# Order of the recurrent blocks, and where the prompt's expert rows stand, in a one-core hybrid diffusion step

## The reference, cut to what matters

```python
def trunk_layer(x, cond, p, cache):
    sh_a, sc_a, g_a, sh_f, sc_f, g_f = adaln(cond, p['w_ada'], p['b_ada'])
    h = rmsnorm(x, p['norm_attn_g']) * (1.0 + sc_a) + sh_a
    q, k, v, xr, xg, ga, gr = jnp.split(h @ p['w_in'], IN_SPLITS, axis=-1)
    ...
    rnn, hf_last, hb_last = rglru_branch(xr, ...)
    a_out = attn @ p['w_attn_o']
    r_out = (rnn * jax.nn.gelu(xg)) @ p['w_rnn_o']
    mix = (jax.nn.sigmoid(ga) * a_out + jax.nn.sigmoid(gr) * r_out) @ p['w_out']
    x = x + g_a * mix
    h = rmsnorm(x, p['norm_ffn_g']) * (1.0 + sc_f) + sh_f
    return x + g_f * peer(h, ...), k, v, hf_last, hb_last

def rglru_dir(xc, w_a, b_a, w_i, b_i, lam, h0, reverse):      # once forward, once backward
    r = jax.nn.sigmoid(blockdiag(xf, w_a) + b_a)
    ig = jax.nn.sigmoid(blockdiag(xf, w_i) + b_i)
    log_a = -LRU_C * r * jax.nn.softplus(-lam)
    a = jnp.exp(log_a)
    bterm = jnp.sqrt(-jnp.expm1(2.0 * log_a)) * ig * xf
    _, h = lax.associative_scan(_lin_combine, (a, bterm), axis=1)

# peer: per token 8 heads x 16 experts = 128 slots
act = gelu(einsum('chkd,cd->chk', u_tab[eidx], x))            # one dot product per slot
out = einsum('chk,chkd->cd', g * act, v_tab[eidx])            # one weighted row per slot
```

## Time and profile before

| what | value |
|---|---|
| median of the runs | 2470.72 us |
| profiled execution | 2466.62 us |
| its span in the profile | 2464.7 us |
| VectorE busy | 1873.9 us (76%) |
| TensorE busy | 1785.5 us (72%) |
| GpSimd busy | 1041.1 us (42%) |
| ScalarE busy | 514.6 us (21%) |
| moved by DMA | 753.43 MB, mean 306 GB/s |

### The profile page before, as it was taken

The page is one execution under the profiler, slowest core; times in us unless marked ns, Lnnn a source line. Parts: engine busy times, 40 slices in busy tenths (PEclk is TensorE's granted clock), DMA queues, the critical chain, the costliest instruction groups (busy, mean ns, idle before and its releaser), DMA issues.

```text
span 2464.7 us, 20335 instructions
## 1 busy us (share of the span) xinstructions
PE 1785.5 (72%) x6013; PEld 1085.0 (44%) x6013; DVE 1873.9 (76%) x3933; ACT 514.6 (21%) x1283; POOL 1041.1 (42%) x1028
## 2 busy tenths in 40 slices
PE   7788889889987989991334666689999997000185
PEld 3578754444456438450012333556666664000032
DVE  2342388875689466899999999888687987999955
ACT  0464113550024000110004555720000000000111
POOL 0000001224534341443775766344344447777674
PEclk9889999999998999996556777899999998555599
DMA  8766774557855595765997999689999999999997
GB/s 278 250 196 209 253 215 149 162 171 268 313 198 187 199 336 168 284 229 201 397 409 290 391 392 387 201 317 411 414 411 406 410 408 411 410 409 410 369 401 308
DMA packets 296873, 753.43 MB, mean 306 GB/s; under 512 B 21502, under 2 KB 141102, under 8 KB 296244
## 3 DMA queue, kind: packets, MB, share of 16 engines
q0 software_dynamic: 147456, 536.94, 57.6%
q1 hardware_dynamic: 149308, 215.20, 24.9%
HBM read 740.72 MB, written 11.33 MB: 305 GB/s over the span
## 4 chain that ended last, share of the span: by engine, by line
DVE 37%; PE 26%; DMA 17%; POOL 8%; issue 7%; ACT 5%; SPq 1%; DVEq 0%; ACTq 0%; POOLq 0%
PE bank L779 8%; PE pair L779 6%; DMA ring_more<-in_peer_u_dram,eidx 6%; DVE attn L1530 5%; DVE big L1530 4%; ACT work L1080 3%; PE bank L960 3%; DVE ring_more L1530 3%; PE bank L1008 3%; POOL attn L2089 2%; DMA attn<-in_peer_u_dram,eidx 2%; POOL big L2089 2%; PE bank L752 2%; DMA big<-in_peer_u_dram,eidx 2%; DMA h_all<-in_peer_u_dram,eidx 2%
## 5 line engine op out<-in xcount | busy, mean ns | idle before, releaser
L1008 PE MATMUL bank<-big,work 128*128 128x512 f32 x192 | 123.9, 781 | 392.9 <-ACT work L1080 269.5
L2089 POOL DMA_INDIRECT h_all<-in_peer_u_dram,eidx x117 | 129.7, 1108 | 569.9 <-DVEq L1958 366.2
L779 PE MATMUL pair<-big 128*128 128x128 f32 (+1 forms) x1280 | 359.3, 438 | 5.1 <-issue 3.6
L779 PE MATMUL bank<-big 128*128 128x512 f32 (+1 forms) x1056 | 312.3, 457 | 20.3 <-DVEq L1399 13.6
L2089 POOL DMA_INDIRECT attn<-in_peer_u_dram,eidx x205 | 201.8, 984 | 238.5 <-DVE dots L1530 167.7
L1053 PE MATMUL bank<-h_all,big 128*128 128x512 f32 x608 | 267.0, 595 | 4.5 <-DMA h_all<-in_peer_v_dram 4.5
L1530 DVE CUSTOM_DVE_ANT_0 attn<-attn,pair 128x1024 f32<-128x1024 f32 x205 | 244.0, 1219 | 32.8 <-DMA attn<-in_peer_u_dram,eidx 28.8
L779 PEld LDWEIGHTS pair<-big 128*128 128x128 f32 x1280 | 196.8, 194 | 154.7 <-issue 152.5
L2089 POOL DMA_INDIRECT ring_more<-in_peer_u_dram,eidx x145 | 156.1, 1077 | 208.6 <-DVE dots L1504 100.1
L1008 PEld LDWEIGHTS bank<-big,work 128*128 128x128 f32 x192 | 41.8, 237 | 456.6 <-issue 419.0
L779 PEld LDWEIGHTS bank<-big 128*128 128x128 f32 x1056 | 173.6, 206 | 154.2 <-issue 146.8
(11 more groups left out here) (310 smaller groups left out, 3020.2 us busy)
## 6 DMA issues: line engine op xcount, KB each, us to landing
big<-in_w_in_dram SPq DMA_DIRECT2D x44, 1024.0 KB, 6.3
h_all<-in_peer_v_dram SPq DMA_DIRECT2D x76, 512.0 KB, 6.8
big<-in_w_ada_dram SPq DMA_DIRECT2D x24, 1024.0 KB, 8.9
big<-in_peer_w_q_dram SPq DMA_DIRECT2D x16, 1024.0 KB, 5.8
gf_row<-in_peer_v_dram SPq DMA_DIRECT2D x26, 512.0 KB, 6.8
work<-in_peer_v_dram SPq DMA_DIRECT2D x26, 512.0 KB, 6.8
big<-in_w_rnn_o_dram SPq DMA_DIRECT2D x8, 1024.0 KB, 6.4
big<-in_w_attn_o_dram SPq DMA_DIRECT2D x8, 1024.0 KB, 6.9
```

The costliest lines, as they stand in the source:

```text
L779: last = nc.tensor.matmul(u[:, 0:n], w[:, k, col:col + P], src[:, k, 0:n], start=(k == 0), stop=(k == KD - 1))
L1008: last = nc.tensor.matmul(psum[i][:, :], diag[:, (n - 1) % DIAGS, :], ring[r][:, i * 512:(i + 1) * 512], start=(k == first_by_tensor[c]), ...
L2089: g.indirect_dma_start(dst, None, ins["peer_" + table][0], bass.IndirectOffsetOnAxis(ap=eidx[:, c, k:k + 1], axis=0)).then_inc(landed, 16)
```

## The change

Nothing of what is computed changes. Six edits:

1. Prompt phase, TensorE: the gates of block j-1 stand between `xr` and `xg` of block j, no longer behind the ada unit.
2. Prompt phase, buffers: `lru_rows` gives odd and even blocks different halves of the buffers (a prompt block uses 128 of 512 columns), so ScalarE's wait for `lru_done` reaches back two blocks, not one.
3. ScalarE: `gelu_in` is split. `gelu_tanh(j + 1)` stands behind the six exp-type instructions of block j in both phases; `gelu_square(j + 1)` moves there too in the prompt phase and keeps its place for the latents.
4. VectorE: the second gelu step becomes `gelu_out`, and stands behind the four products of the block before.
5. Latents, `serve`: two items per recurrent block (before: five, counting the one in `conv`); 7 and not 4 ahead of the recurrent merge, and 9 and not 5 beside each of its steps.
6. Latents, `serve`: none beside the last two queries; 2 + 1 per attention quad (before: 3 + 1).

Of the first 133 items the recurrent stage now does 16, the merge 7 + 72, the queries 12, attention 24, and two are left for `gelu_dots(0)`.

```diff
@@ units
             unit((ph, "xr", j), 2 * (j % 2))
+            if ph == 0 and j:
+                gates(j - 1)
             unit((ph, "xg", j), 2 * (j % 2) + 1)
...
-            if j:
+            elif j:
                 gates(j - 1)
@@ buffers
-        lt, la, le, lth, lti = ([wk(2 + 2 * i), wk(3 + 2 * i)] for i in range(5))
+        def lru_rows(ph, j):
+            c0 = (j % 2) * P if ph == 0 else 0
+            return ([wk(2 + 2 * i + d)[:, c0:c0 + TOK[ph]] for d in range(2)] for i in range(5))
@@ ScalarE
-                    if j + 1 < LB:
-                        gelu_in(j + 1)
+                    if ph and j + 1 < LB:
+                        gelu_square(j + 1)
...
-                    if j:
+                    if ph and j:
                         act.wait_ge(lru_done, B)
+                    if ph == 0 and j >= 2:
+                        act.wait_ge(lru_done, B - 1)
...
+                    if j + 1 < LB:
+                        if ph == 0:
+                            gelu_square(j + 1)
+                        gelu_tanh(j + 1)
                     for d in range(2):
                         act.wait_ge(w_ready, 2 * B + d + 1)
@@ VectorE
-                    serve(1)
+                    serve(0)
+
+                def gelu_out(j):
...
                     if j + 1 < LB:
                         conv(j + 1)
-                    serve(1)
...
-                        serve(1)
+                    serve(1)
+                    if j + 1 < LB:
+                        gelu_out(j + 1)
...
-                        serve(5 if a == "gr" else 5)
-                serve(4)
+                        serve(9 if a == "gr" else 5)
+                serve(7)
...
                         rope((ph, "q", h), featT[:, h, 0:N])
-                        serve(2)
+                        if h < NH - 2:
+                            serve(2)
...
-                    serve(3)
+                    serve(2)
                     dve.wait_ge(prob_ready, G * Q + G)
```

More of the change, by code:

```diff
@@ L370, in hybrid_step @@
         xc = [wk(0), wk(1)]
-        lt, la, le, lth, lti = ([wk(2 + 2 * i), wk(3 + 2 * i)] for i in range(5))
+        assert TOK[0] == P
+        def lru_rows(ph, j):
+            c0 = (j % 2) * P if ph == 0 else 0
+            return ([wk(2 + 2 * i + d)[:, c0:c0 + TOK[ph]] for d in range(2)] for i in range(5))
         sm_pair = [wk(4 * i, 4).rearrange("p (h n) -> p h n", h=G) for i in range(2)]
@@ L1138, in _, with gelu_square, gelu_tanh @@
                     end_stage()
-                def gelu_in(j):
+                def gelu_square(j):
                     u = full((ph, "xg", j))
                     run(featT[:, j, 0:N], u[:, 0:N], ACT.Square).then_inc(sq_ready, 1)
+                def gelu_tanh(j):
                     act.wait_ge(cub_ready, LB * ph + j + 1)
                     run(featT[:, j, 0:N], featT[:, j, 0:N], ACT.Tanh, scale=GELU_C * GELU_S).then_inc(gtanh_ready, 1)
-                gelu_in(0)
+                gelu_square(0)
+                gelu_tanh(0)
                 for j in range(LB):
                     B = LB * ph + j
-                    if j + 1 < LB:
-                        gelu_in(j + 1)
+                    lt, la, le, lth, lti = lru_rows(ph, j)
+                    if ph and j + 1 < LB:
+                        gelu_square(j + 1)
                     i = j + 1 - (LB - NKV)
@@ L1762, in conv @@
                     V.scalar_tensor_tensor(f, f, 1.0 / GELU_C, g[:, 0:N], ALU.add, ALU.mult).then_inc(cub_ready, 1)
-                    serve(1)
+                    serve(0)
+                def gelu_out(j):
+                    B = LB * ph + j
+                    g, f = full((ph, "xg", j)), featT[:, j, 0:N]
                     dve.wait_ge(gtanh_ready, B + 1)
@@ L1772, in _ @@
                 conv(0)
+                gelu_out(0)
                 for j in range(LB):
                     B = LB * ph + j
+                    lt, la, le, lth, lti = lru_rows(ph, j)
                     if j + 1 < LB:
                         conv(j + 1)
-                    serve(1)
                     y = xc[j % 2][:, 0:N]
```

## The result

The changed kernel takes 2483.03 us (median of 5 runs, 2479.44 to 2486.54), the kernel before 2470.72: a ratio of 1.0053, interval 1.0039 to 1.0066. Run again beside its variants on another chip it gave 1.0071 (1.0057 to 1.0084). The forecast was 2462.5 us, with a range of 2437 to 2482.

The account below looks back on a forecast made before the run. Bounds: a ring of waits (prompt), VectorE (latents' recurrent stage, attention), TensorE then expert-row supply (merge). Terms -17 + 16.6 - 7.8 = -8.2 us, the 16.6 including the latents' -18.6, gave 2462.5 us; range 2437 to 2482.

Parts of the forecast that it names:

- Prompt's recurrent stage, -17: Prompt's recurrent stage, edits 1 to 4: engines run a block ahead, 9.0 us per block, stage ends at 154.5, not 171.4.
- ring of waits: Prompt's recurrent stage before: TensorE stops 2.58 us for a bank VectorE frees, waits running through three engines, none of them full.
- the ada tiles (1.5 each): Prompt's recurrent stage: TensorE would wait some 1.5 us per pair of blocks for an ada weight tile landing late.
- the input (2.4): Prompt's recurrent stage: latents' input, with rotary tables and masks, delays the fifth block's tile; 2.4 us once, between 0 and 4.
- Latents' recurrent stage, -18.6: Latents' recurrent stage, edits 3 to 5: VectorE's block drops under TensorE's 17.2 us, so merge outputs start 18.6 us earlier.
- Merge and queries with 79 rows: Recurrent merge and queries, edits 5 and 6: row supply through five buffers delays attention to 723.9, +16.6 with the -18.6 included.
- Attention, -7.8: Attention, edit 6: one row fewer ahead of the output bank's release in seven quads, 7.8 us saved.
- (a): Rival, merge and queries: expert rows keep up at 1.47 us each throughout; -36 us in all, 2434.6; chance 0.22.
- (b): Rival, recurrent merge steps: waiting for rows replaces VectorE's own work; at 2.17 us per row +15 us, 2485.7; chance 0.15.
- (c): Rival, prompt's stage: ring exchanged for ScalarE's own chain through costlier function table changes; -8.7 there, 2470.8 in all; chance 0.13.

Follow-up runs that it names:

- early rotation: Changed kernel with the rotation of the two k units back in VectorE's convolution step, behind the first gelu step, not in gelu_out; ratio 1.0007 to the kernel before.
- the input late: Changed kernel with the latents' input, rotary tables and mask requested later, ahead of the third gr tile; ratio 1.0091 to the kernel before, 2489.2 us.

## Why the prediction was wrong

- **Prompt's recurrent stage, -17: right in its limit, wrong in the wait, 3 us short** (-14.0 at the `ro` outputs). The ring of waits is gone and tiles are what TensorE waits for, as forecast. But the waits were put at the ada tiles (1.5 each) and the input (2.4), 6.9 in all; they stand ahead of `xr`, for the `xg` tile, and are 2.08 + 2.85 + 1.51 = 6.4, and the input costs next to nothing. That the two sums are close is luck. What was missing is TensorE at its lower clock behind two of the waits, 1.7 us each, 3.4 in all, and five waits of 0.17 to 0.20 us for ScalarE. With the clock the six blocks are 56.4 - 0.5 + 3.4 = 59.3 of the 60.4 measured, and the small waits are the rest.
- **Latents' recurrent stage, -18.6: this is the step that failed.** The prediction made the stage, from its first unit on, TensorE's own time: 20 units and 8 gates, with no wait for a bank. That holds for blocks 0 to 5, and VectorE's block of 15.6 us is met (blocks 2, 3 and 4 end 15.5 and 15.7 us apart with the early rotation). It fails in the last two blocks, where I counted on moving the second gelu step alone, and not on what stood behind it in the same function and moved along: the rotations that free the banks of `xr(7)` and `gr(0)`. TensorE's waits for these banks, put at nothing, are 10.96 and 7.53 us, and the lower clock behind them costs another 5.5. Shown by the early rotation: 216.9 becomes 192.9, which is 211.5 - 18.6. The size is 24.0 us of the stage.
- **Merge and queries with 79 rows:** right in the main. 178 us forecast (723.9 less 545.8), 174.9 measured, and 182.5 once the stage ahead is as forecast; for the row price 1.85 on average forecast, 1.90 found; TensorE's first stall, 11.73 us, comes at the seventh `ro` bank, forecast for the sixth. That loaded steps are slow and later ones fast (1.97, then 1.65) was not so: steps of 14.5, 18.2, 15.8, 16.3, 15.3, 20.0 and 14.5 us. My reason, that only five rows are out at a time, is half shown: a sixth helps, but less than in proportion.
- **Attention, -7.8:** -7.4 measured.
- **Sum.** Forecast -8.2 of the span; -14.4 + 5.4 + 31.9 - 7.4 + 1.2 = +16.6 measured (the sum of rounded terms is 16.7). With the stage at 192.9 the same terms give -7.3, nearly my figure. But that is not what the kernel with the early rotation does: 7.6 us come back in the merge, and its ratio is 1.0007 (0.9990 to 1.0024), where the forecast's 2462.5 us would be 0.9967. So the failed step accounts for the larger part of the miss, and not for all of it.
- **Rivals.** (a) is out: 1.90 and not 1.47 us per row. (b), slower by a row price of 1.96 or more, has the sign but not the cause: the price was lower, and the loss came from a bank. (c) did not happen: TensorE waits for ScalarE in the prompt's stage by 0.20 us at a time, ahead of the ada unit. I had no rival for the two blocks in which TensorE has four units and not two, though the changed kernel's text shows the rotation standing in `gelu_out`.

## What to carry to other kernels

When a step is moved out of a function, list what stands behind it and moves along, above all what frees a buffer: here three VectorE instructions behind a wait for ScalarE kept TensorE waiting 11 us for a bank. Small work that hides in gaps has two limits, and both are to be counted: how fast it is supplied, and the engine's own work on it behind the last thing the other engine waits for. Here 60 rows beside merge and queries took 143.0 us, 69 took 147.6 to 149.6 and 85 took 167.0, over TensorE's own 137.5; with 85 it was three rows beside each query that made VectorE end late. Shedding work from the busiest engine gains only with the ring of waits cut as well: here fewer rows alone gave nothing, and order, early rotation, 69 rows and a sixth buffer together 37 us. And a wait should stand where its data is needed: TensorE waits for the `xg` tile ahead of `xr`, where only the `xr` tile is needed; what that costs was not measured.

## What the runs showed of the hardware

- One more buffer for gathered rows of 4 KB per partition raises the rate of all transfers, weight tiles included, from 304 to 342 to 368 GB/s with four, five and six, and the landing of a row takes longer for it (6.0 us with four, 7.7 with six).
- A pause of about 2 us in a light stage of TensorE can be followed by a stretch at the lower of its two levels, 1.2 and not 2.4 GHz (granted clock 0.50 from 90.2 to 93.5 us, 0.72 over 89 to 95): a wait of 2 us then costs nearly 4. The wait's length alone does not tell: with the input late, the clock stayed at 1.00 behind 1.98 and 2.06 us and was 0.72 behind 1.85. Behind the waits of 10.96 and 7.53 us it was 0.50 too, and these cost 24.0 us together and not 18.5.
- The kernel before took 2537 us on one chip and 2468 on others. Nearly all of such a difference lies behind the start of the `mix` matmuls: from there, the four kernels traced on that chip take 1607 to 1617 us, the others 1540 to 1547. Why is open.
